# A two-layer hybrid encoder on one core: the residual seeds the experts' sums, one unit of weights gets a place outside the slots, and queries and keys are projected transposed

## The reference

```python
for i in range(DEPTH):                                   # 2
    hn = rms_norm(h, norm_mix[i])
    mix = even_mixer(...) if i % 2 == 0 else odd_mixer(...)
    h = h + mix
    h = h + hierarchical_moe(rms_norm(h, norm_ffn[i]), ...)
    gate = sigmoid(rms_norm(h, norm_ple[i]) @ ple_w_gate[i])
    h = h + gate * (p[i] @ ple_w_proj[i])
return rms_norm(h, final_norm)
```

```python
sc  = einsum('bnihd,bnjhd->bnhij', qc, kb) * (d ** -0.5) + bias
pr  = softmax(where(mask, sc, NEG_INF));   o = pr @ vb
```

## Time and profile before

| | us |
|---|---|
| median of 3 timed runs | 753.59 (753.17 to 754.75) |
| the profiled execution's own time | 756.25 |
| its span, first to last instruction | 754.2 |
| TensorE busy | 721.3 (96%) |
| VectorE, ScalarE, GpSimd busy | 277.1, 145.2, 27.0 |
| moved by DMA | 250.86 MB, 333 GB/s on average |

### The profile page before, as it was taken

How to read it: one execution, slowest core, us unless ns; L and a number is a source line. 1 busy time by engine, 2 the same in 40 slices (tenths; PEclk the granted TensorE clock), 3 DMA queues, 4 the chain that set the end, 5 groups by cost and what they waited for, 6 DMA issues and landing times.

```text
span 754.2 us, 8201 instructions
## 1 busy us (share of the span) xinstructions
PE 721.3 (96%) x3102; PEld 328.0 (43%) x3102; DVE 277.1 (37%) x662; ACT 145.2 (19%) x355; POOL 27.0 (4%) x49
## 2 busy tenths in 40 slices
PE   9899999999999999979999999999999999988996
PEld 6345454564333333323445554564333333332344
DVE  1213352364326242322322464263525423233233
ACT  3000241331111111100221143232111111110032
POOL 2400000000000000000000000000000000000000
PEclk9999999999999999999999999999999999999999
DMA  9996437839999999999999980357999999999941
GB/s 345 274 359 252 195 145 297 350 122 403 420 422 422 420 421 421 421 421 420 400 335 239 422 330 5 124 211 275 423 421 421 420 421 421 421 421 421 408 181 56
DMA packets 50408, 250.86 MB, mean 333 GB/s; under 512 B 4712, under 2 KB 5832, under 8 KB 25536
## 3 DMA queue, kind: packets, MB, share of 16 engines
q1 hardware_dynamic: 48000, 244.97, 82.3%
q0 software_dynamic: 2048, 5.07, 2.1%
q10 hardware_dynamic: 320, 0.29, 0.1%
HBM read 247.14 MB, written 4.73 MB: 334 GB/s over the span
## 4 chain that ended last, share of the span: by engine, by line
PE 67%; DMA 18%; SPq 7%; issue 2%; DVE 2%; ACT 1%; POOLq 0%; POOL 0%; DVEq 0%; ACTq 0%
PE bank L631 25%; PE bank L907 19%; PE bank L924 9%; DMA weights<-in_moe_w_up_dram 7%; DMA weights<-in_moe_w_down_dram 7%; SPq L421 7%; DMA weights<-in_even_w_in_dram 4%; PE bank L937 3%; PE bank L884 2%; PE bank L617 1%; PE bank L916 1%; PE bank L835 1%; PE bank L1122 1%; PE bank L1134 1%; PE bank L1124 0%
## 5 line engine op out<-in xcount | busy, mean ns | idle before, releaser
L907 PE MATMUL bank<-weights,expert_rows 128*64 128x512 f32 x1024 | 227.9, 594 | 13.7 <-DMA weights<-in_moe_w_up_dram 13.7
L631 PE MATMUL bank<-weights,normalised 128*128 128x512 f32 (+1 forms) x512 | 219.3, 582 | 4.3 <-DMA weights<-in_even_w_in_dram 3.7
L907 PEld LDWEIGHTS bank<-weights,expert_rows 128*64 128x64 f32 x1024 | 75.2, 137 | 157.5 <-issue 156.8
L631 PEld LDWEIGHTS bank<-weights,normalised 128*128 128x128 f32 x512 | 95.0, 190 | 109.5 <-issue 107.1
L924 PE MATMUL bank<-weights,hidden_turned 128*64 128x512 f32 x256 | 58.8, 598 | 1.3 <-DVE hidden_turned L1791 0.6
L924 PE MATMUL bank<-weights,hidden_turned_odd 128*64 128x512 f32 x256 | 58.8, 598 | 0.6 <-DMA weights<-in_moe_w_down_dram 0.6
L1368 ACT ACTIVATE gate_tanh<-bank 128x256 f32<-128x256 f32 x32 | 12.3, 384 | 198.6 <-PE bank L907 198.6
L1233 ACT ACTIVATE expert_outputs<-bank 128x512 fp32r<-128x512 f32 x32 | 19.1, 597 | 123.8 <-PE bank L924 123.8
L1821 DVE TENSOR_TENSOR gather_onehots<-bank,expert_outputs 128x512 fp32r<-128x512 f32 x32 | 22.1, 692 | 55.4 <-ACT expert_outputs L1233 55.3
L1791 DVE COPY hidden_turned<-bank 128x256 f32<-128x256 f32 x16 | 6.8, 424 | 84.4 <-PE bank L916 84.4
L1791 DVE COPY hidden_turned_odd<-bank 128x256 f32<-128x256 f32 x16 | 6.8, 425 | 80.9 <-PE bank L916 80.8
(11 more groups left out here) (249 smaller groups left out, 583.3 us busy)
## 6 DMA issues: line engine op xcount, KB each, us to landing
weights<-in_moe_w_gate_dram SPq DMA_DIRECT2D x64, 1024.0 KB, 19.7
weights<-in_moe_w_up_dram SPq DMA_DIRECT2D x64, 1024.0 KB, 21.4
weights<-in_moe_w_down_dram SPq DMA_DIRECT2D x64, 1024.0 KB, 22.4
weights<-in_even_w_in_dram SPq DMA_DIRECT2D x5, 2048.0 KB, 32.6
weights<-in_ple_w_gate_dram SPq DMA_DIRECT2D x4, 2048.0 KB, 31.2
weights<-in_even_w_out_dram SPq DMA_DIRECT2D x2, 2048.0 KB, 19.5
weights<-in_odd_w_qkv_dram SPq DMA_DIRECT2D x2, 2048.0 KB, 22.7
weights<-in_odd_w_out_dram SPq DMA_DIRECT2D x4, 1024.0 KB, 22.0
```

Source lines behind the costliest of these rows:

```text
L631: mm = pe.matmul(B[bank][:, 0:width], XT[:, k, tok(t)], w[:, k, :], start=(k == 0), stop=(k == KD - 1))
L907: mm = pe.matmul(bank[j * BLK:(j + 1) * BLK, :].rearrange("p (m f) -> p m f", m=2), rows[:, k, :], W[:, slots, a:a + FF // 2], start=(k == ...
```

## The change

Three things are edited.

1. *Sums seeded with the residual.* The four banks of the experts' sums are renumbered: `sum_bank(t, half)` is 2 (1 - t) + half. They are opened with a product of zeros (`open_sums`), tokens 0 before the first expert's rows and tokens 1 in the middle of expert 2's gate and up products. ScalarE then writes `H` into them (`seed`), and every scatter adds. After the last expert VectorE copies the banks to `H` (`summed_rows`) and no longer adds.
2. *Expert 2's down weights outside the slots.* `H` is then free during the experts. The unit goes, per partition, half into a new tile `XD` (whose second half is also the second part of the side weights), a quarter into `H[:, 0]` and a quarter into `H[:, 1]`. To make room, several SBUF tiles are dropped or laid over others. The other units keep their order and move one slot position forward; SP's order in the turns of experts 3 and 5 is changed.
3. *Queries and keys of the attention projected transposed* (`turned_unit`): the weights are stationary and the moving operand is `XT`, 256 tokens. The two `turn` calls for them are gone. Keys are scaled on the way out by a row of `rstd` that two small products spread over the partitions (`rstd_row`); queries stay unscaled, and `scale0` uses `rstd * HD ** -0.5` per token.

```diff
-MOE_SLOTS = ((2, 3, 4, 5, 6, 7, 8, 0, 1), (3, 4, 5, 6, 0, 7, 8, 1, 2))
-BETWEEN_SLOTS, END_SLOTS = (5, 6, 0, 7, 8, 1, 2), (6, 0, 7)
+MOE_SLOTS = (2, 3, 4, 5, 6, 7, 8, 0, 1)
+BETWEEN_SLOTS, END_SLOTS = (4, 5, 6, 7, 8, 0, 1), (4, 5, 6)
+OUTSIDE = (U_MOE0 + 8, U_MOE1 + 8)
...
+                def outside(f):
+                    s = srcs[2][l * NE + 2][256 * (f // 2):256 * (f // 2) + 256, :].rearrange("(p c) d -> p c d", c=2)
+                    sp.dma_start(H[:, f - 2, :], s[:, f - 2, :]).then_inc(sem("down2_rest_landed"), 16)
...                                  # SP, expert 3's turn, behind the stores of the side product
+                        sp.wait_ge(sem("side_second_stored"), 32 * (l + 1))
+                        sp.dma_start(XD[:, :], srcs[2][l * NE + 2][0:256, :].rearrange("(p c) d -> p (c d)", c=2))\
+                            .then_inc(sem("down2_landed"), 16)
+                        sp.wait_ge(sem("seeded"), 4 * l + 2)
+                        outside(2)
                         for half in range(2):
                             load_part(3, 1, half)
-                            load_part(2, 2, half)
                             load_part(4, 0, half)
                             load_part(4, 1, half)
-                        load_down(3)
+                            load_part(3, 2, half)
+                    elif e == 5:
+                        load_part(5, 0, 0)
+                        load_part(5, 0, 1)
+                        load_part(5, 1, 0)
+                        sp.wait_ge(sem("seeded"), 4 * l + 4)
+                        outside(3)
+                        load_part(5, 1, 1)
+                        load_down(4)
...                                  # TensorE, even mixer
+            def turned_unit(u, pair):
+                if pair == 0:
+                    s, v = landed(U_IN + u)
+                    pe.wait_ge(s, v)
+                pe.wait_ge(sem("in_by_act" if pair else "in_by_dve"), u - 1)
+                w = unit(U_IN + u).rearrange("p (k n) -> p k n", k=KD)
+                for c in range(2):
+                    for k in range(KD):
+                        mm = pe.matmul(B[2 * (u % 2) + pair][:, c * SEQ:(c + 1) * SEQ], w[:, k, tok(2 * pair + c)],
+                                       XT[:, k, :], start=(k == 0), stop=(k == KD - 1))
+                mm.then_inc(sem("in_ready"), 1)
+            def rstd_row():
+                for t in range(TT):
+                    mm = pe.matmul(B[4][:, tok(t)], rstd(0, t).to_broadcast([P, P]), ident, start=True, stop=True)
+                mm.then_inc(sem("rqk_turned"), 1)
...
-            in_unit(2, 0)
+            turned_unit(2, 0)
             pe.wait_ge(sem("ret_rotated"), 2)
             turn(RRO, (4, 5), "rqk_turned")
-            in_unit(2, 1)
+            turned_unit(2, 1)
             retention_scores()
-            in_unit(3, 0)
+            turned_unit(3, 0)
             retention_values()
-            in_unit(3, 1)
-            ...
-            turn(STG[1], (4, 5), "aqk_turned")
-            in_unit(4, 0)
-            ...
-            turn(STG[0], (4, 5), "aqk_turned")
-            in_unit(4, 1)
+            rstd_row()
+            turned_unit(3, 1)
+            in_unit(4, 0)
+            in_unit(4, 1)
+            pe.wait_ge(sem("in_by_dve"), 5)
             ...
             scores0(0)
...                                  # TensorE, experts
+                def open_sums(t):
+                    for half in range(2):
+                        r = slice(64 * half, 64 * half + 64)
+                        mm = pe.matmul(B[sum_bank(t, half)][:, :], ZERO[r, 0:1].to_broadcast([64, P]),
+                                       ZERO[r, 0:1].to_broadcast([64, 512]), start=True, stop=False)
+                    mm.then_inc(sem("sums_open"), 1)
...                                  # second_half(e, n), inside gate_up
+                    if e == 2:
+                        pe.wait_ge(sem("act_ready"), NE * l + 2)
+                        open_sums(1)
                     wait_second(n, n + 1)
...                                  # scattered(e)
-                    scatter(e % 2, e == 2, 0)
+                    if e == 2:
+                        pe.wait_ge(sem("seeded"), 4 * (l + 1))
+                    scatter(e % 2, 0)
...                                  # step(e), the down product
-                        wait_unit(n)
+                        if n in OUTSIDE:
+                            pe.wait_ge(sem("down2_landed"), 16 * (l + 1))
+                        else:
+                            wait_unit(n)
...                                  # its second half: waits down2_rest_landed for that unit
                 gathered(1, 0)
+                pe.wait_ge(sem("rows_by_act"), 4 * l + 2)
+                pe.wait_ge(sem("rows_by_dve"), 4 * l + 2)
+                open_sums(0)
                 first_rows(0)
...                                  # ScalarE
+                def seed(t):
+                    act.wait_ge(sem("sums_open"), 2 * l + t + 1)
+                    for half in range(2):
+                        copy(B[sum_bank(t, half)][:, :], H[:, t, half * 512:(half + 1) * 512]).then_inc(sem("seeded"), 1)
...                                  # seed(0) behind the two small exponentials, seed(1) behind
...                                  # the copy of expert 0's output in step(1)
...                                  # VectorE
+            def summed_rows(t, half):
+                dve.tensor_copy(H[:, t, half * 512:(half + 1) * 512], B[sum_bank(t, half)][:, :]).then_inc(sem("h_updates"), 1)
...                                  # behind the retention's decays
+            dve.wait_ge(sem("rqk_turned"), 3)
+            then(dve.tensor_copy(RSTD_ROW, B[4][:, 0:SEQ]))
+            keys_evac(0)
```

189 lines of the change are left out of this document (98 added, 91 removed).

## The result

Four timed runs of the changed kernel gave 746.39 to 748.79 us, median 747.49; four of the kernel before 753.17 to 754.75, median 753.54. The ratio of changed to before is 0.9907, with a 95% interval of 0.9883 to 0.993. The forecast was 745.7 us, with 742.5 to 749.5 as its range. The changed kernel run again gave a median of 746.85 beside 754.0, ratio 0.9899 (0.9865 to 0.9933).

What follows compares the result with a forecast made beforehand. TensorE, busy 96% of the span, was taken as the bound, its idle time late in each layer's experts set by transfers at 421 GB/s. Terms -7.5 + 0.8 - 1.2 = -7.9 from 753.59 gave 745.7 us, range 742.5 to 749.5.

Steps and rivals of the forecast that it cites:

- The signs that I had named: Up-weight waits about 7 us, 1.5 MB before the slots' stream, layer 0's last down piece near 359 us, scores 1.2 us sooner.
- Step 1: Expert 2's down weights outside the slots: 1.5 MiB moved ahead in an empty queue, 3.7 us a layer, -7.5 us in all.
- Rival A: The early transfers also bridge the stream's restart after the pause: up to 5.6 us a layer, 742.0 us; chance 0.14.
- Step 2: Last quarter of expert 2's down weights, into H[:, 1] inside expert 5's loads: cost 0, with 8 us to spare.
- a dent after 190 us: Sign of a wrong forecast: the weight stream's rate drops around the last quarter's transfer into H[:, 1].
- Rival B: Only part of the 1.5 MiB is won, H's quarters at half rate or late: 748.1 us; chance 0.12, including 747.5 to 752.
- Step 3: Opening the sums' banks with two pairs of small matmuls per layer: +0.4 us a layer, +0.8 us in all.
- Step 5: Even queries and keys projected transposed: transposes -1.76 us, row of rstd +0.5, 256-column instructions +0.1, together -1.2 us.
- rival D: Weight loads of the transposed projection not hidden: slower, 770.0 us if fully exposed; chance 0.06 with anything else slower.
- Steps 4 and 6: Copies replacing additions after the sums, and small VectorE or GpSimd edits: 0 us, bounds 0.1 and 0.3 us.

Runs made afterwards that it cites:

- rows in blocks: The changed kernel with expert 2's down rows taken in blocks of 128 rows, so transfers read HBM without gaps; 746.18 us, ratio 0.99 to the kernel before.
- the first kernel with the seeds alone: The changed kernel with expert 2's down weights back in the slots, but the changed kernel's slot lists kept; 771.34 us.
- the second kernel with the seeds alone: The changed kernel with expert 2's down weights back in the slots and every unit's slot as in the kernel before; 753.61 us, ratio 0.9988.

## Why the prediction was right, and where it was off

*The bound* was read rightly. Early bytes shorten a layer at the queue's rate, bytes in the stream don't, and seeds alone do nothing. The signs that I had named came: 7.0 us of waits, 1.5 MB in the 7 us ahead of the slots' stream (220 GB/s), the first scores 1.1 us sooner, counted from unit 2's first product. The last down piece of layer 0 was 1 us late: TensorE goes on at 357.64, and with the 2.77 us by which unit 2's products start sooner in this profile that is 360.4, for 359.

*Step 1, the tenth place,* forecast 3.74 us a layer. Measured by stretches in the first two profiles 2.8 and 3.7; with the second pair of profiles as well the means are 3.2 and 3.9, 7.2 us in all for 7.5. The first pair gave 6.5. XD was issued 2.0 us before the first expert product, as worked out (159.6 against 161.6). Its 1.5 MiB did go ahead (246 GB/s over the 4 us in which there had been 2), and the restart didn't get better by it: from 3 to 16 us behind the first expert product the slots' pieces of 8 KB come to 4.1 MB in the kernel before and in the changed one, and the 345 GB/s for 317 there are the rest of H[:, 0]. Rival A had no part. The yardstick has 33 GB/s, 1.42 MB, of the 1.57 MB; what is missing fits the window around 190 us, and with rows in blocks it is 37 GB/s, 1.59 MB. The forecast had no term for the pieces of the next transfer that get ahead of the last landing. In layer 0 of the changed kernel's first profile they are 0.85 MB for 0.59 in the first profile of before, and that is 0.6 us of the 0.9 by which that stretch missed its 3.74.

*Step 2, H[:, 1].* Issue at 186.57 us, 28.5 behind the first product (forecast: 28.6), and TensorE never waited for it. But I had named a dent after 190 us as a sign of error, and there is one: 391 for 421 over 6 us, 0.4 us. It falls on the 4 KB pieces and is absent without gaps, but also absent in one kernel with them, so its cause is open. Rival B's half rate was about true (199 to 248 GB/s in four profiles), and its price was not, as the transfer lay in idle time.

*Step 3, opening.* 0.41 us from 157.69 to 158.10, twice: +0.8, exact.

*Step 5, the projection.* -1.1 and -0.7 with the opening, for -1.2. The row of rstd took 62.88 to 63.33, 0.45 for the forecast 0.5, and a unit's 32 products 7.1, so rival D is out. The rule of the Trainium skill that I had weighed there ("TensorE: Matmul & The Clock Gate", Part 3, overlap only for differing row groups) is contradicted by 128 loads of 190 ns beside full-array products: 32 of them and their products fit in 7.1 us. Part 2 of that page of the Trainium skill also allows a load ahead into a background weight buffer, and with that the trace agrees.

*Steps 4 and 6* at 0: the stretch between the layers' experts is 0.38 longer, 0.41 of it the opening, the tail the same.

*The sum.* By stretches, means of both profiles each: -0.71, -3.25, +0.39, -3.93 and +0.04, together -7.5; by the timed medians -6.1 in the first comparison and -7.2 in the second. The forecast was -7.9. The mis-sized term is that of step 1, by 0.3 us with all four profiles and by 1.0 with the first two. In the first comparison the forecast was off by 1.8 us; the part that step 1 doesn't cover most likely is the start: waits for unit 2 of 0.5 to 3.7 us in fourteen profiles move whole runs. I had worked from one profile and taken its 2.66 us above the median as something that cancels in a difference. In a difference of two profiles it didn't (9.6 us); in my forecast, which subtracted from the median, it did.

## What to carry to other kernels

Where a queue bounds the end of a long stretch, count the bytes that it has moved at the point from which it never pauses: a buffer that can be filled in the pause before is worth its bytes at the queue's rate, and the same buffer filled later is worth nothing. Ask of a dip in the rate whether filling it changes the sum at that point: here it came back 5 us later. Where engines wait for the last transfer of a long row, count also the pieces of the next transfer that have got ahead of it; they made 0.7 us between two runs of one kernel. And a list of slots is part of a change: take one unit out of a ring, or put one in, and every place behind it needs to be counted again.

## What was not expected of the hardware

The end of a row of transfers is not sharp: when the last down piece landed, 0.50 to 1.02 MB of the transfer behind it had already moved, in 22 stretches of eleven profiles.

Pieces of 4 KB with gaps of 12 KB between them left 232 GB/s over 3 us in which the queue had work; with pieces without gaps in that place it was 371 over the first 2 of them. Out of an empty queue, from 1.0 to 3.0 us behind the issue, 4 KB pieces had 227 and 242 GB/s with gaps of 4 KB and 264 to 276 without, 8 KB pieces 270 to 299; one microsecond on all had 401 or more.

TensorE's clock fell after three of the waits. In the first kernel with the seeds alone it was idle for 7.56 us, and was granted half its speed, 1.2 GHz, for some 10 us from within the wait on. Eight products that take 3.5 us took 6.55. The second such wait, 7.03 us in layer 1, went the same way (0.50 in the window from 730 to 734 us).

```profile
375.74 6.55 PE L639 MATMUL bank<-weights,normalised 128*128 128x512 f32 x8 [7.56 <-DMA weights<-in_ple_w_gate_dram]
```

```profile
370.00:374.00 4.00, 0.00 (x0) 0.00 (x0) 0.15 (x1) 0.39 (x2) 0.56 (x1) 0.66 1.03 411
374.00:378.00 4.00, 2.26 (x3) 1.18 (x4) 0.00 (x0) 0.00 (x0) 0.00 (x0) 0.50 1.05 389
378.00:382.00 4.00, 4.00 (x6) 1.53 (x5) 0.00 (x0) 0.00 (x0) 0.00 (x0) 0.56 1.04 407
```

In the second kernel with the seeds alone, a start with a wait of 3.17 us was followed by a clock of 0.66 and 0.77 in two windows of 3 us, and the first projection took 8.86 us for 7.17. That is the 1.7 us by which its first stretch is longer:

```profile
38.38:41.38 3.00, 3.00 (x9) 2.52 (x10) 0.00 (x0) 0.00 (x0) 0.00 (x0) 0.66 1.04 394
41.38:44.38 3.00, 3.00 (x12) 2.44 (x12) 0.00 (x0) 0.00 (x0) 0.00 (x0) 0.77 1.04 364
```

The first profile of before had a wait of 3.67 us in the same place and kept a clock of 1.00. So a late first transfer can cost twice, by the wait and by the clock after it; of the fourteen profiles one shows it.
